# A fused inference step with page turns, score groups and key transposes moved by one to two half tiles

## What is computed

```python
# shared keys and values, from the residual x after the retention layer
kv = rmsnorm(x, kv_norm_w) @ w_kv                    # 1024 -> 2 * 1024
k, v = jnp.split(kv, 2, axis=-1)
k = rmsnorm(k.reshape(B, T, 8, 128), k_norm_w)       # stored as an output, and used
# attention of the sampled tokens, for each sequence
k_s = concatenate([cache_k[pages], k_new]); v_s = concatenate([cache_v[pages], v_new])
p = softmax(q @ k_s.T + bias(distance), masked)      # per head
out = (p @ v_s) * silu(gate) @ moba_w_out + x
```

## Time and profile before

| | us |
|---|---|
| median of 3 executions | 502.35 (501.89 to 503.01) |
| the profiled execution | 500.89 |
| its span | 498.9 |
| PE busy | 490.5 (98%) |
| DVE busy | 357.7 (72%) |
| ACT busy | 260.6 (52%) |

### The profile page before, as it was taken

The page is one execution under the profiler, slowest core; times in us unless marked ns, Lnnn a source line. Parts: engine busy times, 40 slices in busy tenths (PEclk is TensorE's granted clock), DMA queues, the critical chain, the costliest instruction groups (busy, mean ns, idle before and its releaser), DMA issues.

```text
span 498.9 us, 9903 instructions
## 1 busy us (share of the span) xinstructions
PE 490.5 (98%) x3689; PEld 424.8 (85%) x3689; DVE 357.7 (72%) x633; ACT 260.6 (52%) x536; POOL 96.8 (19%) x139
## 2 busy tenths in 40 slices
PE   8999999999999999999999999999989999999997
PEld 6989978899788996799799999987757778999885
DVE  3865529894598829896389987998956764776662
ACT  5826533465417724475454364764737655556630
POOL 0292002720063200930000042446002000000000
PEclk9999999999999999999999999999999999999999
DMA  8993988999899998999956899999998467683211
GB/s 267 326 339 135 254 283 274 373 365 249 260 335 396 267 222 312 349 360 234 265 163 216 293 301 210 268 234 201 265 300 282 152 220 237 233 300 133 85 53 53
DMA packets 86770, 125.54 MB, mean 252 GB/s; under 512 B 5491, under 2 KB 51524, under 8 KB 86596
## 3 DMA queue, kind: packets, MB, share of 16 engines
q1 hardware_dynamic: 85874, 124.63, 82.2%
q0 software_dynamic: 768, 0.28, 0.4%
q10 hardware_dynamic: 82, 0.02, 0.0%
HBM read 98.93 MB, written 27.57 MB: 254 GB/s over the span
## 4 chain that ended last, share of the span: by engine, by line
PE 92%; DVE 3%; ACT 2%; issue 1%; DMA 0%; POOL 0%; DVEq 0%; ACTq 0%; POOLq 0%
PE bank L941 46%; PE bank L938 18%; PE bank L922 7%; PE bank L1050 3%; PE bank L1170 2%; PE bank L1064 1%; PE bank L997 1%; PE bank L1112 1%; PE bank L1216 1%; ACT rows L1505 1%; PE bank L877 1%; DVE small L1738 1%; PE bank L1030 1%; PE bank L1031 1%; PE bank L1032 1%
## 5 line engine op out<-in xcount | busy, mean ns | idle before, releaser
L1580 DVE TENSOR_TENSOR w_lo<-w_raw,w_hi 128x512 fp32r<-128x512 f32 x207 | 143.9, 733 | 64.0 <-ACT w_hi L1240 63.2
L1240 ACT ACTIVATE w_hi<-w_raw 128x512 fp32r<-128x512 f32 x208 | 118.5, 620 | 65.3 <-PE bank L941 34.8
L941 PE MATMUL bank<-xn_hi,w_hi 128*128 128x320 f32 x320 | 100.1, 317 | 0.7 <-ACT w_hi L1240 0.7
L941 PE MATMUL bank<-xn_hi,w_lo 128*128 128x320 f32 x320 | 97.7, 309 | 0.1
L941 PE MATMUL bank<-xn_lo,w_hi 128*128 128x320 f32 x320 | 97.6, 309 | 0.0
L938 PE MATMUL bank<-w_hi,xn_hi 128*128 128x512 f32 x160 | 64.8, 405 | 0.0
L941 PEld LDWEIGHTS bank<-xn_hi,w_hi 128*128 128x128 f32 x320 | 59.7, 188 | 4.7 <-issue 2.9
L938 PE MATMUL bank<-w_lo,xn_hi 128*128 128x512 f32 x160 | 62.5, 391 | 0.0
L938 PE MATMUL bank<-w_hi,xn_lo 128*128 128x512 f32 x160 | 62.4, 390 | 0.0
L941 PE MATMUL bank<-ym_hi,w_hi 128*128 128x320 f32 x192 | 60.9, 317 | 0.0
L941 PEld LDWEIGHTS bank<-xn_lo,w_hi 128*128 128x128 f32 x320 | 59.8, 188 | 0.4 <-DVE xn_lo L1629 0.2
(11 more groups left out here) (291 smaller groups left out, 782.4 us busy)
## 6 DMA issues: line engine op xcount, KB each, us to landing
w_raw<-in_ret_w_in SPq DMA_DIRECT2D x23, 1024.0 KB, 11.2
st<-in_state_ret SPq DMA_DIRECT2D x32, 512.0 KB, 8.3
out_ret_state_sample<-st SPq DMA_DIRECT2D x32, 512.0 KB, 4.6
w_raw<-in_ret_w_out SPq DMA_DIRECT2D x8, 1024.0 KB, 8.6
w_raw<-in_moba_w_in SPq DMA_DIRECT2D x8, 1024.0 KB, 6.2
w_raw<-in_w_kv SPq DMA_DIRECT2D x8, 1024.0 KB, 8.8
cache<-in_cache_v SPq DMA_DIRECT2D x16, 512.0 KB, 4.8
cache<-in_cache_k SPq DMA_DIRECT2D x44, 128.0 KB, 5.2
```

The costliest lines, as they stand in the source:

```text
L941: mm = pe.matmul(bank[out][:, 0:T], w[:, wk, P * tile:P * tile + P], x[:, k, :], **flags)
L1240: act.activation(w_hi[:, c % 2, part], w_raw[:, c % RAW, part], ACT.Copy).then_inc(w_hi_done, 1)
L1580: dve.tensor_tensor(w_lo[:, c % 2, part], w_raw[:, c % RAW, part], w_hi[:, c % 2, part].bitcast(F32), ALU.subtract).then_inc(w_lo_done, 1)
```

## The change

Only places in the list of steps are changed. Turn 11 of the cached key pages goes from place 10 to 12, turn 12 from 12 to 13, turn 13 from 13 to 14; the other turns stay. Score groups 2 and 3 go from places 17 and 21 to 19 and 23. KX 0 and 1 go from 15 and 16 to 16 and 17. SE 1 goes from 22 to 24, the middle of v0's first tile.

```diff
-    for n, at in enumerate((0, 1, 3, 4, 5, 5, 6, 8, 9, 10, 12, 13, 15, 16)):
+    for n, at in enumerate((0, 1, 3, 4, 5, 5, 6, 8, 9, 12, 13, 14, 15, 16)):
         g[at].append(("KP", n + 2))
     g[4].append(("QT",))
     g[4].append(("KS", 0))
-    for q, at in enumerate((9, 17, 21)):
+    for q, at in enumerate((9, 19, 23)):
         g[at].insert(0, ("KS", q + 1))
     for n, at in enumerate((8, 10, 11, 20, 22, 23)):
         g[at].append(("KN", n))
     g[11].append(("SE", 0))
-    g[22].append(("SE", 1))
-    g[15].insert(0, ("KX", 0))
-    g[16].insert(0, ("KX", 1))
+    g[24].append(("SE", 1))
+    g[16].insert(0, ("KX", 0))
+    g[17].insert(0, ("KX", 1))
     g[26].append(("KX", 2))
     g[27].append(("KX", 3))
```

## The result

The changed kernel took 507.73 us in the median of eight executions (505.58 to 508.97), the kernel before 502.31 beside it (eight, 501.89 to 505.17). The ratio is 1.0087 with an interval of 1.0063 to 1.0111: slower, by 3.2 to 5.6 us. Its profiled execution took 505.58 us with a span of 503.6, against 500.89 and 498.9. The forecast was 504.8 with 502.7 to 508.2 around it.

A forecast was written before the change was run, and what follows sets the result against it. TensorE, busy 98% of the span, was taken as the bound. L1227 at 370.3 plus 11.6 and 2.3 put KX 2 at 384.2, 2.4 us later, which moved the 502.35 us median to 504.8, range 502.7 to 508.2.

The forecast's parts named there:

- The sign: Whole kernel: slower than before, with KX 2 and the end 2.4 us later; chance of slower 0.74.
- both mechanisms: Late key stores hold ACT's copy L1227 until 370.3; SE 1 behind two splits holds KX 2 2.3 us past KN 5.
- Rival A: Key stores don't hold L1227; only SE 1's place binds, KX 2 about 382.4, 503.0 us, no difference; chance 0.17.
- rival B: PE's arrival sets KX 2, both pauses go, KX 2 1.3 us earlier, 501.0 us; chance 0.06.
- KX 0's pause and that inside group 2: PE's pauses of 0.31 us before KX 0 and 1.66 us inside score group 2, both taken as gone.
- rival C: Key stores land slowly, 7 to 8.1 us; KX 2 at 386.8 to 387.9, about 508 us; chance 0.13.
- the forecast's own case: Stores hold L1227 and SE 1 holds KX 2, giving 503.4 to 506.3 us; chance 0.52.
- Rival D: PE idle 3.9 us before KX 2 drops the clock to the 1.2 GHz level; about 507 us; chance 0.12.
- The sum KX 2 = L1227 + 13.9: KX 2 starts 11.6 plus 2.3 us behind L1227 at 370.3: 384.2 against 381.76, 2.4 us later.
- Issue of the stores: SP issues the first key store at 364.6, the last starts near 365.9: 4.45 us later than before.
- Landing: Last key store, started about 365.9, lands by bytes in the queue at 370.3; bounds 369.4 to 374.0.
- With some loss for small waits: DVE's fourth low split of the third key chunk ends at about 364.1 as before; PE waits some 1.2 us.

The follow-up runs named there:

- after, stores first: Changed kernel with the first half's three key stores issued at turn 12's step, ahead of page 15's load; 503.70 us, ratio 1.0008.
- before, stores first: Kernel before with only the first half's key stores moved to turn 12's step, ahead of page 15's load; 503.33 us against 502.65, ratio 1.0007.
- filler kernel: Changed kernel with SE 1 at place 23, key stores ahead of page 15's load, 14 useless matmuls in PE's long pause; 501.10 us, ratio 0.9957.
- before, SE 1 at 24: Kernel before with SE 1 alone moved from place 22 to 24; 505.67 us against 503.76, ratio 1.0038.
- before, turns moved: Kernel before with turns 11 to 13 alone moved to places 12, 13 and 14; 503.92 us against 503.76, ratio 0.9992.
- after again: Changed kernel run once more, unedited, beside the kernel before; 506.53 us against 503.67, ratio 1.0071.
- turns back: Changed kernel with turns 11 to 13 at their old places 10, 12 and 13; 506.91 us, ratio 1.0077.
- SE 1 at 23: Changed kernel with SE 1 at place 23 instead of 24; 503.96 us, ratio 1.0018.
- turns back, SE 1 at 23: Changed kernel with turns 11 to 13 at their old places and SE 1 at place 23; 503.28 us, ratio 0.9993.
- late turns, stores first: Changed kernel, turns 11 to 13 back, SE 1 at 23, turns 14 and 15 at 17 and 19, key stores before page 15's load; 498.02 us, ratio 0.9886.
- late turns: Changed kernel with turns 11 to 13 back, SE 1 at 23, turns 14 and 15 at places 17 and 19; 502.59 us, ratio 0.9986.

## Why the prediction was right, and where it was not

**The sign and both mechanisms held.** KX 2 was held by SE 1's first operation, which ended half of its 0.87 us pair behind 385.87, at 386.3; KN 5 ended at 382.62 + 1.28 = 383.90. That is 2.4 us, forecast 2.3. L1227 was held by the stores, shown by "after, stores first" and by "before, stores first", and by the landings: in eleven of the 14 traces the copy starts about 0.1 us or less behind the landing of the last store, and in the other three ("after, stores first", the filler kernel and "before, stores first"), where the store had landed 1.1 to 3.0 us earlier, right behind the matmul that filled its bank. Rival A (stores don't hold) falls with them, rival B with "before, SE 1 at 24". No gain came back behind KX 2: 117.11 against 117.14. KX 0's pause and that inside group 2 went, as forecast. The landing of 7 to 8 us that rival C wanted did not occur: 5.4, 6.5 and 5.7 us in the three traces with this order on SP.

**The size was too small**, +2.4 where the segment shows +4.45. The profiled execution, 505.58, and the median, 507.73, stand against 503.3 and 504.8; the median is inside the range, but above the forecast's own case (503.4 to 506.3), where rivals C and D had been put. That it is inside is owed to the room left for them and not to the sum, which forecast about half of what was lost. The sum KX 2 = L1227 + 13.9 was off by 0.3; the error is nearly all in L1227, 370.3 forecast and 372.31 measured, 0.28 of it from ahead of the stretch.

- *Issue of the stores.* Forecast 364.6 and the last near 365.9; measured 365.67 and about 366.9. Turn 11 ended at 359.75 (forecast 359.54) and page 15 was first issued at 360.49 (forecast 360.30), but its four issues took 2.86 us instead of 2.00, and so value page 16 followed at 364.13 where 363.1 was reckoned.
- *Landing.* Forecast 4.4 us, measured up to 5.4. Page 15 was taken to land at about 365.5, for which no row stood; its last part, issued at 361.99, landed after 4.5 us, at 366.5. In the 14 traces the last store landed 13.3 to 14.3 us into the segment with only page 14 and the weight chunk shortly ahead of the stores on SP, 16.9 to 19.0 with page 15 and value page 16 too, and 18.3 to 20.3 with value page 17 as well. The time of issue moved along with these loads, so the two aren't fully separated; behind the same loads, an issue 4.4 us later ("before, turns moved" against before) moved the landing by 2.1. Within one order the landing differed by about 1 us from trace to trace, so the prediction's sum by bytes could not have been exact.

**A step was missing.** I wrote that page 15's load moves and that the weight load "is now issued some 2.5 us earlier and is gone from the queue". The same shift put page 14's load, which hangs on turn 11's step, behind that 1 MB load: SP issued chunk v0 at 352.91 and page 14 from 354.08 to 355.96. In the kernel before it had issued page 14 at nearly the same time, 353.83 to 355.38, but ahead of the chunk, and its four parts landed in 3.4 us in the median; now it was 7.8, and 8.8 for the last. Turn 14 waited 2.19 us for the page, the fourth low split started at 365.96 where I had it end at 364.1, and PE paused 3.74 us instead of 1.2. I had looked for DVE's order and not for the page that one of its steps waits for; "With some loss for small waits" was the sentence that failed. PE reached KX 2 at 385.06 instead of 380.3: some 2.5 us by this pause, and as much by what it set off.

**Rival D came true at another place.** I had priced a fall of the clock for the pause before KX 2 and gave it 0.12. It came ahead of group 2, since that pause was long: the granted clock fell to the 1.2 GHz level, 0.50 of full speed, for about 6 us (0.68 in the mean of the ten us from 366 to 376), which cost 2.5 us on PE. The Trainium skill, "TensorE: Matmul & The Clock Gate", section "Why this matters for your kernels", warns of gaps between bursts of matmuls. The rows agree, with pauses of 3.7 to 4.5 us in five traces (after, after again, turns back, SE 1 at 23, stores first), each followed by a stretch at 0.50, and with the filler kernel, in which it stayed at 1.00.

**Two chains meet at KX 2**, and this is why no term can be subtracted alone: PE's (late split, low clock) arrives at 385.06, SE 1's lets it start at 386.49. Taking SE 1 away gave 1.0 to 1.6 us in the trace, taking the stores away 0.7 to 1.3, and in both PE's chain was left bare. Only with early splits, SE 1 ahead, early stores and late turns together did the segment fall under that of before.

**The median lost more than the trace.** The table gives the 95 executions of the kernel before that the experiments were compared with, by mean granted clock:

| mean clock | executions | median us |
|---|---|---|
| 0.999 and over | 30 | 501.85 |
| 0.995 to 0.998 | 50 | 503.50 |
| under 0.995 | 15 | 504.94 |

So in two of three executions the kernel before had a clock that was not at its upper level throughout, and these took 1.6 to 3.1 us longer in the median; the order is the same on each of the four chips. That the clock is the cause is argued from the traces above and was not tested here. The one trace of the kernel before, at 1.000, shows the good case. The changed kernel was at 0.993 or under in 15 of 17 executions; "turns back, SE 1 at 23" was at 0.999 or over in all ten. Where in the stretch the kernel before loses its clock, no trace shows: this is open. So is why "late turns, stores first" gained 4.7 us in the median and 2.4 in the trace; the clock accounts for part (against executions of before at 0.999 and over on its chip, 501.54 from four, it is 3.5 us).

**Still open** is also what the pause inside group 2 is (the prediction counts 256 matmuls there; they are 128, with 128 weight loads). It had no releaser in five traces (1.66, 2.48, 0.46, 0.41 and 1.92 us) and was absent in the others. That PE's instructions arrive late there fits: in all five the pause ends 2.7 to 2.9 us behind a 16 KB packet on PE's instruction queue, however long it is. But no experiment addressed it.

## What to carry to other kernels

When a step is moved in a hand-written order, list for every engine and queue what the step issues and what those transfers now stand behind; a load that slips behind one 1 MB chunk can hold an unrelated split. Behind the same loads, a store issued 4.4 us later landed only 2.1 us later here; with the loads taken out from ahead of it ("before, stores first" against before) an issue 3.7 us earlier landed 3.3 us earlier. So move work out from ahead of a transfer, and don't count an earlier issue in full. A wait of TensorE can cost twice, by its length and by the clock behind it: read the granted clock behind every wait of a few us, shorten the wait or fill it, and compare a kernel's mean granted clock over many executions before you trust one trace.

## What was not expected of the hardware

- With 14 useless matmuls (3.3 us) in a 3.9 us wait, PE needed 15.94 us for the instructions behind it; without them it needed 18.40, 18.19 and 18.51 us in three traces.
- The length of a pause alone doesn't tell whether the clock falls. In "before, turns moved" it fell to 0.57 (384 to 388) behind a pause of 2.12 us, with another of 1.54 us 4.5 us ahead of it, and in "late turns" to 0.61 (376 to 380) behind one of 2.01 us, with no other but 0.41 us, 8 us ahead. In "before, SE 1 at 24" it stayed at 1.00 with pauses of 2.48 and 2.27 us that stood 17 us apart. What decides it these runs don't show.
- The slowest of the first half's key stores took between 5.4 and 8.9 us to land in the 14 traces, and up to 1.5 us more or less with the same order on SP (6.8 and 8.3; 5.4, 5.7 and 6.5).
